# Latent attention: the keys' sum of squares as two single-pass products instead of one fp32 product

## The reference

```python
def _rmsnorm(x, gain):
    xf = x.astype(jnp.float32)
    y = xf * lax.rsqrt(jnp.mean(xf * xf, axis=-1, keepdims=True) + RMS_EPS)
    return (y * gain.astype(jnp.float32)).astype(x.dtype)
...
    k_nope, v = jnp.split(kv, [MLA_NOPE], axis=-1)
    k = jnp.concatenate(
        [k_nope, jnp.broadcast_to(k_rope[:, :, None, :], (B, S, MLA_HEADS, MLA_ROPE))], axis=-1)
    q = _rope_tail(_rmsnorm(q, q_norm), cos, sin)
    k = _rope_tail(_rmsnorm(k, k_norm), cos, sin)
    o = _causal_block_attention(q, k, v)
    return o.reshape(B, S, MLA_HEADS * MLA_V_HEAD) @ w_out
```

## Time and profile before

| what | value |
|---|---|
| median of 3 runs | 2018.97 us (2017.87 to 2019.06) |
| the profiled execution | 2018.65 us, of it span 2016.9 us |
| TensorE busy | 1986.4 us, 98% of the span |
| VectorE, ScalarE, GpSimd busy | 976.5, 941.4, 861.0 us |
| granted TensorE clock over the span | 0.996 |
| HBM traffic | 88 GB/s over the span |

### The profile page before, as it was taken

How to read it: one execution, slowest core, us unless ns; L and a number is a source line. 1 busy time by engine, 2 the same in 40 slices (tenths; PEclk the granted TensorE clock), 3 DMA queues, 4 the chain that set the end, 5 groups by cost and what they waited for, 6 DMA issues and landing times.

```text
span 2016.9 us, 26525 instructions
## 1 busy us (share of the span) xinstructions
PE 1986.4 (98%) x10887; PEld 1621.0 (80%) x10887; DVE 976.5 (48%) x1510; ACT 941.4 (47%) x1322; POOL 861.0 (43%) x670
## 2 busy tenths in 40 slices
PE   8999999999999999899999999999999999999999
PEld 7788888878888887677777888888878788888887
DVE  6644443254202216899994553255167645522551
ACT  6666663353223224566664543244267645432441
POOL 2344334526444543443334444444431255444443
PEclk9999999999999999899999999999999999999999
DMA  7122222223232231121212223232210222222231
GB/s 259 53 94 74 73 73 94 94 74 105 97 102 94 94 104 53 64 75 64 75 64 94 94 95 104 84 105 94 89 48 27 79 94 95 97 101 91 98 101 66
DMA packets 51816, 178.30 MB, mean 88 GB/s; under 512 B 5744, under 2 KB 8944, under 8 KB 51568
## 3 DMA queue, kind: packets, MB, share of 16 engines
q1 hardware_dynamic: 51696, 176.61, 25.8%
HBM read 174.49 MB, written 2.10 MB: 88 GB/s over the span
## 4 chain that ended last, share of the span: by engine, by line
PE 92%; DVE 5%; ACT 2%; issue 1%; DMA 0%; POOL 0%; SPq 0%; DVEq 0%; ACTq 0%; POOLq 0%
PE ps_gemm L228 24%; PE ps_gemm L230 24%; PE ps_gemm L229 24%; PE ps_attend L228 4%; PE ps_attend L230 4%; PE ps_attend L229 4%; PE ps_attend L897 1%; PE ps_attend L1758 1%; PE ps_attend L2599 1%; PE ps_attend L2666 1%; PE ps_attend L2601 0%; PE ps_attend L2600 0%; PE ps_attend L910 0%; PE ps_gemm L1726 0%; PE ps_attend L285 0%
## 5 line engine op out<-in xcount | busy, mean ns | idle before, releaser
L2879 POOL TENSOR_TENSOR weights_low<-weights_raw,weights_high 128x512 fp32r<-128x512 f32 (+1 forms) x331 | 432.4, 1306 | 1110.9 <-ACT weights_high L203 1110.7
L228 PE MATMUL ps_gemm<-normed_high,weights_high 128*128 128x512 f32 x1665 | 659.3, 396 | 5.0 <-ACT normed_high L1259 2.6
L230 PE MATMUL ps_gemm<-normed_low,weights_high 128*128 128x512 f32 x1665 | 648.1, 389 | 0.0
L229 PE MATMUL ps_gemm<-normed_high,weights_low 128*128 128x512 f32 x1665 | 647.7, 389 | 0.0
L203 ACT ACTIVATE weights_high<-weights_raw 128x1024 fp32r<-128x1024 f32 (+1 forms) x340 | 339.5, 1006 | 447.3 <-PE ps_attend L230 216.2
L2880 POOL TENSOR_TENSOR weights_low<-weights_raw,weights_high 128x512 fp32r<-128x512 f32 (+1 forms) x331 | 439.1, 1327 | 0.0
L228 PEld LDWEIGHTS ps_gemm<-normed_high,weights_high 128*128 128x128 f32 x1665 | 313.6, 188 | 74.5 <-issue 3.5
L230 PEld LDWEIGHTS ps_gemm<-normed_low,weights_high 128*128 128x128 f32 x1665 | 313.6, 188 | 65.4
L229 PEld LDWEIGHTS ps_gemm<-normed_high,weights_low 128*128 128x128 f32 x1665 | 313.9, 189 | 63.6 <-issue 1.9
L228 PE MATMUL ps_gemm<-operands_high_low,weights_high 128*128 128x512 f32 (+1 forms) x552 | 216.1, 391 | 0.8 <-ACT weights_high L203 0.3
L230 PE MATMUL ps_gemm<-operands_high_low,weights_high 128*128 128x512 f32 (+1 forms) x552 | 214.1, 388 | 0.0
(11 more groups left out here) (335 smaller groups left out, 2167.3 us busy)
## 6 DMA issues: line engine op xcount, KB each, us to landing
weights_raw<-weights_full SPq DMA_DIRECT2D x317, 512.0 KB, 3.3
weights_raw<-weights_short SPq DMA_DIRECT2D x24, 128.0 KB, 2.0
residual<-x_tiles SPq DMA_DIRECT2D x4, 512.0 KB, 8.1
out_tiles<-residual SPq DMA_DIRECT2D x8, 256.0 KB, 2.1
parameters<-params SPq DMA_DIRECT2D x1, 1559.5 KB, 11.5
scratch<-memory_tiles SPq DMA_DIRECT2D x2, 256.0 KB, 5.0
scratch<-memory_tiles SPq DMA_DIRECT2D x1, 512.0 KB, 6.5
scratch<-positions SPq DMA_DIRECT2D x1, 256.0 KB, 11.6
```

The costliest lines, as they stand in the source:

```text
L228: t.op.matmul(out, m.wh[:, c:c + P], xh, start=start and n == 0, stop=False, skip_group_check=True)
L229: t.op.matmul(out, m.wl[:, c:c + P], xh, start=False, stop=False, skip_group_check=True)
L230: ins = t.op.matmul(out, m.wh[:, c:c + P], xl, start=False, stop=stop and n == len(pairs) - 1, skip_group_check=True)
L2879: g.op.tensor_tensor(m.wl[:, a], m.raw[:, a], m.wh[:, a].bitcast(F32), ALU.subtract)
```

## The change

The squares of the keys, summed with those of the rotary part (`sum_k`), are split in a high part (a Copy by ScalarE to fp32r, `sum_k_high`) and a low part (a subtraction by VectorE, `sum_k_low`), which go to the tiles with number 7 of `normed_high` and `normed_low`. The product `total_k` becomes two products in fp32r with a matrix of ones that ScalarE copies to fp32r once. The waits follow: TensorE waits for `sum_k_low`, ScalarE's squares of the next head wait for `sum_k_low` of the one before, and the new Copy waits for `sum_k` and for the earlier `total_k`. The new Copy is the last instruction of `act_front`, the subtraction the last of `dve_front`.

```diff
         self.pt = m.big[:, 12 * TILE + ZW:12 * TILE + 2 * ZW]
-        self.ident, self.mask = m.nl[:, 0:P], m.nl[:, P:2 * P]
+        self.ident, self.mask, self.ones = m.nl[:, 0:P], m.nl[:, P:2 * P], m.nl[:, 2 * P:3 * P]
+        self.sqk_parts = parts(7)
...
     s.op.activation(x.ident, m.col("ident", 0, P), ACT.Copy)
+    s.op.activation(x.ones, m.col("ones", 0, P), ACT.Copy)
...
         if name == "k":
             if h:
-                s.wait_ge(*m.T.at("mla", "total_k", h - 1))
+                s.wait_ge(*m.V.at("mla", "sum_k_low", h - 1))
             s.op.activation(x.sqk, m.gb(2), ACT.Square).then_inc(*m.A.mark("mla", "square_k", h))
...
             s.op.activation(x.sqr[R128, :], m.gb(1)[R128, :], ACT.Square).then_inc(*m.A.mark("mla", "square_r", h))
+    s.wait_ge(*m.V.at("mla", "sum_k", h))
+    if h:
+        s.wait_ge(*m.T.at("mla", "total_k", h - 1))
+    s.op.activation(x.sqk_parts[0], x.sqk, ACT.Copy).then_inc(*m.A.mark("mla", "sum_k_high", h))
...
     if h == 0:
         sum_k()
+    hi, lo = x.sqk_parts
+    v.wait_ge(*m.A.at("mla", "sum_k_high", h))
+    v.op.tensor_tensor(lo, x.sqk, hi.bitcast(F32), ALU.subtract).then_inc(*m.V.mark("mla", "sum_k_low", h))
...
-    t.wait_ge(*m.V.at("mla", "sum_k", h))
+    t.wait_ge(*m.V.at("mla", "sum_k_low", h))
     t.wait_ge(*(m.A.at("mla", "rstd_k", h - 1) if h else m.A.at("mla", "key_rope")))
-    pe_sum_over_partitions(m, t, ("mla", "total_k", h), m.gb(3), x.sqk)
+    pe_split_sum(m, t, ("mla", "total_k", h), m.gb(3), x.ones, x.sqk_parts)
```

## The result

The changed kernel takes 2037.91 us (median of 5 runs, 2034.75 to 2038.12); the kernel before took 2018.2 us in the same measurement. The ratio is 1.0091, with a 95% interval from 1.008 to 1.0102: slower by 19.7 us. The profiled execution took 2038.08 us, its span is 2036.3 us, 19.4 us more than before.

What follows compares the result with a forecast made beforehand. It took the heads to be bound by a loop closed through VectorE, despite TensorE's 98%. Loop 10.8 plus start 0.8 gave 11.6 us, clock 4.8 more: 16.4 us, median 2035.4 us, range 2028.5 to 2041.

Steps and rivals of the forecast that it cites:

- The loop: Heads 0 to 5: scores wait for the low part, 15.16 us apart in heads 1 to 4; 10.8 us altogether.
- The start: Heads 0 and 1: later product in head 0, +0.6 us, and ScalarE standing at its new wait, +0.2; together +0.8.
- the earlier trace: The same two-part sum in the recurrence, at 858.77 us: 0.58 us to the next work, used to price the pair.
- The clock: TensorE's six new waits in the heads: granted clock falls after three, 1.6 us each, +4.8 us.
- ScalarE's Copy: Each head: the new Copy delays that of the probabilities by 0 to 0.1 us, covered by the longer wait.
- A full clock: Rival in the heads: the same wait, but the clock stays full; 2030.6 us, chance 0.29.
- Partly hidden: Rival in the heads: sum_k_low comes about 1 us earlier, loss halved; +3 to +9 us, chance 0.07.
- No change: Rival in the heads: pair and total_q fit beside the wait for ScalarE's Copy of the probabilities; 2019.0 us, chance 0.04.
- TensorE as the bound: Rival in the heads: TensorE bounds, so the shorter pair saves 3.0 us; 2016.0 us, chance 0.04.

Runs made afterwards that it cites:

- the clock kept: The changed kernel with eight extra fp32r products, results overwritten, on TensorE in the wait before total_k: 2029.84 us, ratio 1.0052.
- all the work but not the wait: The changed kernel with Copy and subtraction kept, but TensorE waits for sum_k alone and multiplies the unsplit sum in fp32: 2021.44 us, ratio 1.0014.
- the wait alone: The kernel before, with TensorE's total_k also waiting for VectorE's rotated and no instruction added: 2030.79 us, ratio 1.0057.
- the product made shorter: The kernel before, with the keys' squares in fp32r and total_k as one fp32r product, low part left out: 2016.94 us, ratio 0.9995.
- both orders, clock kept: The changed kernel with subtraction ahead of rotated, total_q ahead of total_k, and three overwritten fp32r products before total_q's wait: 2024.97 us, ratio 1.0031.
- both orders: The changed kernel with the subtraction ahead of rotated on VectorE and total_q ahead of total_k on TensorE: 2024.14 us, ratio 1.0032.

## Why the prediction was right

**The loop.** The mechanism holds: the subtraction starts 0.66 us behind `rotated`, TensorE 0.04 to 0.06 us behind its end. Predicted 15.16 us between scores with a full clock, measured 15.09 to 15.11. The pair took 0.66 us from its start to `total_q` instead of 0.58, since its first product runs 0.50 us behind a wait; `total_q` gave back 0.07, with 0.36 instead of 0.43, and `rotated` came at S + 12.66 instead of 12.76. With the clock kept, the first scores of heads 0 and 6 are 90.39 us apart against 79.61 before. That is 10.8 us more, the sum of the prediction, and to that digit it is luck: each of heads 1 to 4 came out 0.05 to 0.07 us shorter than forecast, and head 5 0.28 us longer (15.73 against 15.45), as the subtraction took 1.00 us there and not 0.68.

**The start.** Predicted 0.8 (0.6 in head 0, 0.2 behind it); the first scores of head 0 come 1.96 us later, of which 1.03 is there already at the product of the key's rotation (L2398, in the changed kernel L2400: it starts at 1494.34 before, 1495.37 after). So 0.93 us is the start's own, 0.7 of it in the sum of head 0 and 0.2 in that of head 1. The earlier part was in no term. 0.48 of it is there already at the place of the earlier trace rows in the recurrence (858.77 before, 859.25 after), which the change does not touch. What the whole of it is was not tested, but the same product starts at 1492.44 in the kernel with the subtraction ahead of `rotated`, which has the same instructions up to there as the changed one, so differences of up to 3 us ahead of the heads need no difference of the kernels.

**The clock.** That it would fall in these waits was right, and it was the larger doubt. The size per fall was taken as 1.6 us and is 1.4. Their number was taken as three of six and was five in the profiled execution. This is the mis-sized term: 4.8 us forecast, 7.2 measured. No row gave the number of falls; three was a guess. The range did not rest on it: six falls of 1.4 us on 2030.6 us would be 2039.0, still inside. No term had head 6 either, which is half a microsecond shorter behind the longer wait (15.86 us without a fall, 16.39 before). The median lies 2.5 us above the forecast of 2035.4.

The account in the profiled spans: 1.03 ahead of the heads, 0.93 in the start, 10.78 by the loop, -0.53 in head 6, 7.20 by the clock. Sum 19.41, and the spans differ by 19.4. Against the 16.4 forecast beside the profiled execution that is 3.0 us more: 2.4 by the clock, 1.0 ahead of the heads, 0.1 in the start, -0.5 in head 6.

**ScalarE's Copy.** Put at 0 to 0.1 us a head without its cover; the kernel with all the work but not the wait shows 0.18, and 0.5 in head 5. In the heads of the changed kernel the longer wait hides it, as was said.

**The rivals.** A full clock: the fastest run of the changed kernel (2034.75) is still 4.9 us above the 2029.84 us that the kept clock gives, which points to falls in all of its runs; as only one of them has a profile, and times ahead of the heads differ too, that is a hint and no proof. For the profiled one the windows settle it. Partly hidden: out by the spacing. No change, and TensorE as the bound: out by the wait alone, which costs 11.6 us with no work added, and by the product made shorter, which gives nothing in the loop.

## What to carry to other kernels

In this loop a shorter product paid nothing, as its engine waited for another operand right behind it; ahead of the loop, where nothing else was late, each of two shorter products gave 0.6 us. So before splitting a product, look which operand comes last for the *next* instruction on its engine. When a step gets one more producer, ask where that producer stands in its engine's order: here it was written behind `rotated`, for which TensorE's sums do not wait, and that one place cost 0.67 us a head, as much as the new instruction itself. And a wait on TensorE of about 2 us is dearer than it looks, as the clock may fall behind it: filling it with products that are thrown away won back 7 us in the heads.

## What the runs showed of the hardware

Waits in a loop with nearly the same period were followed by a low clock in some heads and not in others. In the profiled executions, of the six waits in front of the sums:

- the changed kernel: five of six (waits 1.7 to 2.7 us; the one without a fall was 2.06 us);
- the same with the fp32 product behind the wait: four of six (2.06 to 2.68 us; those without were 1.73 and 2.17 us);
- the subtraction ahead of `rotated`: three (two behind waits of 1.5 us, one behind 2.67 us);
- `total_q` first: three, each behind two waits of 0.90 to 1.26 us;
- both orders, clock kept: one, behind waits of 0.57 and 1.25 us;
- the wait alone: none, with waits of 1.25 to 1.97 us; both orders: none, with two waits of 1.25 us the longest.

So the length of the single wait does not decide it: 1.5 us had a fall and 1.97 us had none. What decides it in a single head was not settled. Each fall cost 1.4 us. The scatter of the runs does not show it either way: the changed kernel's five runs spread over 3.4 us, the four with the clock kept over 1.5 us, but 19 runs of the kernel before over 5.2 us, and its profiled execution has a clock of 1.00 throughout the heads.

Behind a wait for VectorE, both products took longer to the next start than in the earlier trace rows: the pair 0.66 us instead of 0.58, the fp32 product 1.03 and 1.06 instead of 0.95.
